# A hybrid attention and retention layer: rotated keys stored whole beside their halves, two key tiles moved behind the value tiles, and the order of two splits turned round

## The reference, cut to what matters

```
q = rotary(q.reshape(B, S, H, 256), positions)          # H = 4 retention heads
k = rotary(k.reshape(B, S, H, 256), positions) * 256 ** -0.5
v = v.reshape(B, S, H, 512)
def step(R, chunk):                                     # chunks of 128 tokens, 8 for each head
    qc, kc, vc = chunk
    inner = ((qc @ kc.T) * decay_in) @ vc
    cross = (qc @ R) * xi
    R = R * gamma_c + (kc * zeta).T @ vc                # needs the key with its tokens as rows
    return R, inner + cross
```

## Time and profile before

| what | value |
|---|---|
| time, median of 3 runs | 1659.99 us (1658.79 to 1666.12) |
| profiled execution, its own time | 1659.99 us |
| its span | 1658.2 us |
| TensorE busy | 1601.9 us (97%) |
| VectorE busy | 952.4 us (57%) |
| ScalarE busy | 583.6 us (35%) |
| GpSimd busy | 231.9 us (14%) |
| data moved | 300.72 MB, mean 181 GB/s |

### The profile page before, as it was taken

One profiled execution on the slowest core, in us unless ns is written; L12 is line 12 of the kernel. 1 busy time (PEld: TensorE's weight loads), 2 busy tenths in 40 slices (PEclk: granted clock), 3 DMA queues, 4 the chain that ended last, 5 costly groups with the idle time before them and its releaser, 6 DMA issues.

```text
span 1658.2 us, 20322 instructions
## 1 busy us (share of the span) xinstructions
PE 1601.9 (97%) x7788; PEld 1341.4 (81%) x7788; DVE 952.4 (57%) x1472; ACT 583.6 (35%) x1009; POOL 231.9 (14%) x180
## 2 busy tenths in 40 slices
PE   5999999999999999999999999999799999999998
PEld 4778888888888888888888888787588878888886
DVE  6984444444448766555565555655466665647544
ACT  5443333333343323233343433434243333212111
POOL 2232232222311221212000000000010010000000
PEclk8999999999999999999999999999899999999999
DMA  9032323322232558697564454557987786435322
GB/s 387 25 127 109 113 109 113 116 108 109 108 134 82 186 209 303 241 347 219 198 207 171 163 191 166 186 179 270 346 259 239 246 254 236 161 100 218 140 100 79
DMA packets 156240, 300.72 MB, mean 181 GB/s; under 512 B 10864, under 2 KB 95728, under 8 KB 148208
## 3 DMA queue, kind: packets, MB, share of 16 engines
q1 hardware_dynamic: 145344, 269.20, 46.8%
q0 software_dynamic: 4608, 16.78, 2.5%
q10 hardware_dynamic: 6192, 13.44, 2.5%
HBM read 191.90 MB, written 106.95 MB: 180 GB/s over the span
## 4 chain that ended last, share of the span: by engine, by line
PE 84%; DVE 8%; DMA 4%; ACT 2%; issue 2%; SPq 1%; POOL 0%; DVEq 0%; ACTq 0%; POOLq 0%
PE p_banks L2031 9%; PE p_banks L1989 8%; PE p_banks L1991 8%; PE p_banks L1992 8%; PE p_banks L2062 5%; PE p_banks L1904 5%; PE p_banks L1906 5%; PE p_banks L1905 5%; PE p_banks L2237 4%; PE p_banks L2235 3%; PE p_banks L2236 3%; PE p_banks L2296 2%; PE p_banks L2295 2%; PE p_banks L2294 2%; PE p_banks L2133 2%
## 5 line engine op out<-in xcount | busy, mean ns | idle before, releaser
L1509 DVE TENSOR_TENSOR w_form<-w_pair,w_form 128x512 fp32r<-128x512 f32 x120 | 92.9, 776 | 101.8 <-ACT w_form L1156 100.5
L1156 ACT ACTIVATE w_form<-w_pair 128x512 fp32r<-128x512 f32 x120 | 75.6, 632 | 195.3 <-PE p_banks L1992 187.3
L510 ACT ACTIVATE w_hi<-w_raw 128x1024 fp32r<-128x1024 f32 (+3 forms) x79 | 70.1, 889 | 208.9 <-PE p_banks L2237 99.7
L1904 PE MATMUL p_banks<-h_hi,w_hi 128*128 128x512 f32 x304 | 118.6, 390 | 1.6 <-DVE w_lo L516 1.6
L1905 PE MATMUL p_banks<-h_lo,w_hi 128*128 128x512 f32 x304 | 118.3, 389 | 0.0
L1906 PE MATMUL p_banks<-h_hi,w_lo 128*128 128x512 f32 x304 | 118.3, 389 | 0.0
L516 DVE TENSOR_TENSOR w_lo<-w_raw,w_hi 128x1024 fp32r<-128x1024 f32 (+3 forms) x80 | 92.0, 1154 | 31.9 <-ACT w_hi L510 31.5
L2237 PE MATMUL p_banks<-y_hi,w_lo 128*128 128x512 f32 x256 | 99.6, 389 | 0.0
L2236 PE MATMUL p_banks<-y_lo,w_hi 128*128 128x512 f32 x256 | 99.6, 389 | 0.0
L2235 PE MATMUL p_banks<-y_hi,w_hi 128*128 128x512 f32 x256 | 99.6, 389 | 0.0
L1224 ACT ACTIVATE prob<-p_banks,neg_max 128x128 f32<-128x128 f32 (+3 forms) x64 | 47.5, 742 | 144.4 <-DVE neg_max L1607 144.4
(11 more groups left out here) (293 smaller groups left out, 4303.6 us busy)
## 6 DMA issues: line engine op xcount, KB each, us to landing
w_raw<-in_w_dense SPq DMA_DIRECT2D x45, 512.0 KB, 5.3
w_pair<-in_w_pairs SPq DMA_DIRECT2D x20, 1024.0 KB, 4.9
v_ret<-v_stage POOLq DMA_DIRECT2D x32, 512.0 KB, 3.7
qk_chunk<-qk_chunks SPq DMA_DIRECT2D x32, 512.0 KB, 4.0
v_chunk<-v_ret SPq DMA_DIRECT2D x32, 512.0 KB, 4.6
qk_chunks<-split_stage SPq DMA_DIRECT2D x28, 512.0 KB, 5.9
merge_t<-act_t SPq DMA_DIRECT2D x48, 256.0 KB, 3.6
act_t<-stage SPq DMA_DIRECT2D x40, 256.0 KB, 2.0
```

The source lines that it names most:

```text
L1509: nc.vector.tensor_tensor(self.form[f % FORM_SLOTS][:, 1, :], self.form_source(f), self.form[f % FORM_SLOTS][:, 0, :].bitcast(F32), ALU.su ...
L1904: nc.tensor.matmul(out, w_hi[:, slot, cut], x_hi[:, k, tok], start=(k == ks[0]), stop=False)
```

## The change

Four things change.

1. The rotated key is also stored whole. `store_turned` issues for a key pair two more stores of 512 KB, of `rot[:,0]` before the halves of part 0 and of `rot[:,3]` before those of part 1; a chunk in `qk_chunks` has 10 blocks instead of 8, 640 KB instead of 512 KB. The next tile that writes `rot` waits on DVE until the stores of all key pairs so far have landed (`rot_stored`). SP waits for the same before it loads the first attention gate.
2. `sum_keys`, `k_chunk_full` and `KEY_SUMS` go; TensorE transposes blocks 8 and 9 of the loaded chunk.
3. `x10` and `x11` move behind `v3`: `... x9 k4 v0 k5 v1 k6 v2 k7 v3 x10..x15`. The loads of the first attention operands are issued after x11's stores instead of after v3's.
4. For `q` and `k` tiles ACT and DVE first split the result and then the weight of tile r+3; before it was the other way round.

```diff
@@ -77,8 +77,8 @@
 for n in range(4):
-    SEQ += [("k", 4 + n), ("v", n)] + [("x", 10 + n)] * (n < 2)
-SEQ += [("x", n) for n in range(12, TURNS)]
+    SEQ += [("k", 4 + n), ("v", n)]
+SEQ += [("x", n) for n in range(10, TURNS)]
@@ -108,7 +108,6 @@
-KEY_SUMS = {28: 2, 29: 3, 30: 6}
@@ -192,8 +191,7 @@
-        self.qk = z("qk_chunk", 56, [P, 3, 8, P], F32R)
-        self.k_full = z("k_chunk_full", 68, [P, 3, 2, P])
+        self.qk = z("qk_chunk", 56, [P, 3, 10, P], F32R)
...
@@ -405,7 +403,8 @@
             elif kind in "abx":
-                self.rot_pair[r] = rot // 4
+                self.rot_pair[r], self.k_turns[r] = rot // 4, turned
+                turned += kind == "x" and i % 4 == 3
@@ -673,10 +672,10 @@
-            if r == R_LAST_V + 2:
+            if r == R_LAST_V + 3:
...
@@ -702,6 +701,7 @@
         sp.wait_ge(self.w_lo_ready, R_V + V_PARTS)
+        sp.wait_ge(self.rot_stored, 16 * 2 * H_RET)
@@ -726,6 +726,11 @@
         for part in range(2):
+            if is_k:
+                sp.wait_ge(self.rot_added, 2 * self.rot_pair[r] + part + 1)
+                col = (8 + part) * P
+                sp.dma_start(dst[:, :, col:col + P], self.rot[:, 3 * part, :].rearrange("p (m n) -> p m n", m=NT))\
+                    .then_inc(self.rot_stored, 16)
             sp.wait_ge(self.split_lo_ready, s + part + 1)
...
@@ -1094,15 +1086,13 @@
             if kind in "qk":
-                self.split_weight(act, r + RING)
                 act.wait_ge(*self.done[r])
                 self.split_hi(act, self.splits[r], self.two_banks(r))
...
-            if kind not in "qk":
-                self.split_weight(act, r + RING)
+            self.split_weight(act, r + RING)
@@ -1395,6 +1385,8 @@
             dve.wait_ge(self.split_lo_ready, self.splits[before] + 2)
+            if self.k_turns[r]:
+                dve.wait_ge(self.rot_stored, 32 * self.k_turns[r])
@@ -1525,7 +1517,6 @@
             if kind in "qk":
-                self.lower_weight(dve, r + RING)
                 self.split_low(dve, self.splits[r], self.two_banks(r))
...
-            if kind not in "qk":
-                self.lower_weight(dve, r + RING + (r == R_V - 1))
+            self.lower_weight(dve, r + RING + (r == R_V - 1))
@@ -2141,11 +2131,11 @@
     def turn_keys(self, pe, n):
-        pe.wait_ge(self.k_summed, n + 1)
+        pe.wait_ge(self.chunk_loaded[n % 3], 16 * (n // 3 + 1))
...
-            last = self.nc.tensor.transpose(self.p[:, 5, b * P:(b + 1) * P], self.k_full[:, n % 3, b, :],
+            last = self.nc.tensor.transpose(self.p[:, 5, b * P:(b + 1) * P], self.qk[:, n % 3, 8 + b, :].bitcast(F32),
...
-            "qk": scratch("qk_chunks", (H_RET, NT, P, 8 * P)),
+            "qk": scratch("qk_chunks", (H_RET, NT, P, 10 * P)),
```

More of the change, by code:

```diff
@@ L305, in semaphores @@
         self.rot_added = sem("rot_added")
+        self.rot_stored = sem("rot_stored")
         self.split_stored = [sem("split_stored_%d" % n) for n in range(3)]
@@ L338, in semaphores @@
         self.gc_loaded = [sem("gate_chunk_loaded_%d" % n) for n in range(3)]
-        self.k_summed = sem("k_chunk_summed")
         self.k_turned = sem("k_turned")
@@ L393, in counts @@
         self.done, self.free, self.splits, self.store_count = {}, {}, {}, [0, 0, 0]
-        summed = evicted = split = rot = 0
-        self.rot_pair = {}
+        summed = evicted = split = rot = turned = 0
+        self.rot_pair, self.k_turns = {}, {}
         for r, (kind, i) in enumerate(SEQ[:R_MERGE]):
@@ L675, in sync @@
             kind, i = SEQ[r]
-            if r == R_LAST_V + 2:
+            if r == R_LAST_V + 3:
+                later = [s for s in self.slot_of if s >= self.splits[R_LAST_V + 2]]
                 for n in range(3):
-                    later = [s for s in self.slot_of if s >= self.splits[r] and self.slot_of[s] == n]
-                    sp.wait_ge(self.split_stored[n], self.stores_before[later[0]] if later else self.store_count[n])
+                    sp.wait_ge(self.split_stored[n], self.stores_before[[s for s in later if self.slot_of[s] == n][0]])
                     sp.wait_ge(self.v_up_stored[n], 16 * 4)
@@ L989, in gpsimd @@
                 nc.gpsimd.tensor_tensor(rot[:, 3, :], rot[:, 3, :], rot[:, 1, :], ALU.add).then_inc(self.rot_added, 1)
-        sums = 0
         for unit in range(FILL_UNITS):
-            while sums < KEY_SUMS.get(unit, 0):
-                self.sum_keys(pool, sums)
-                sums += 1
             self.store_fill(pool, unit)
[L996 to L1004, removed]
     def store_fill(self, queue, unit):
```

## The result

The changed kernel takes 1677.17 us (median of 5, 1675.96 to 1679.56), the kernel before 1659.94 (median of 5). The ratio is 1.010, 95% interval 1.008 to 1.012: 17.2 us slower. The forecast was 1671.6 with a range of 1662 to 1680, and slower by more than 0.5%. So the sign and the range held, and the size was 5.6 us short. The forecast's own band, 1667 to 1676, is missed by 1.2 us. That the wide range holds is luck: its upper end, 1680, was the price of a rival that did not occur.

The account below looks back on a forecast made before the run. TensorE, busy 1601.9 of 1658.2 us, was taken as the bound, so only its tile starts count. Terms of 6.4, 1.1, 2.2, 0.9 and 1.0 sum to 11.6 us on 1659.99: 1671.6 us, range 1662 to 1680.

Parts of the forecast that it names:

- The forecast's own band: Range given to the forecast case itself, 1667 to 1676 us, with chance 0.58.
- Part 1 at x4: Up stage: x4's rotary products wait for the whole-row store until 561.0, so x6 starts late; +6.4 us, bounds 4 to 10.
- wait of 2 us at q3: Up stage, expected sign: TensorE has new waits of about 2 us each before q1, q3 and a0.
- Part 4 at x8: Up stage: x8's high weight, now made after the split, delays its start; +1.1 us, bounds 0 to 2.
- Part 3: k and v in a row: v2 waits 3.1 us, v3's 1.8 us stall goes; +2.2 us, bounds -1.8 to +8.
- Part 1 at the end of the up stage: One more store in front of the first value load makes it land later; +0.9 us, bounds 0 to 1.9.
- Part 2: Retention's start: removed POOL sums gain 0, larger chunk loads delay the last set 0 load; +1.0 us, bounds 0 to 1.3.
- 6.4 + 1.1 + 2.2 + 0.9 + 1.0: Sum of the five terms over the whole kernel, 11.6 us slower.
- recovered in between: Rival: only 1 to 3 us remain at x6 and k and v in a row come out even; 1665 us, chance 0.20.
- bound by transfers: Rival: stores in the k and v run are not caught up, costing 8 us and more at x10, x11; 1680, chance 0.15.
- not slower: Rival: the whole-row store lands by 555.5, costing nothing, and -1.8 us remains at v3; 1658 us, chance 0.07.
- signs named beforehand: Expected if right: x4 near 561, x6 6.4 us late, v2 waiting 3 us, v3 none, y_lo waits 1 longer.

Follow-up runs that it names:

- Run 4: The change, with the whole-row store of rot[:,3] issued by ScalarE on its own queue; 1668.64 us, ratio 1.0077 to the kernel before.
- run 6: The change, with spare products that nobody reads on TensorE before q1 and before v2's fifth tile; 1675.6 us, ratio 1.0102 to the kernel before.
- Run 2: The kernel before with only k and v in a row, x10 and x11 moved behind v3; 1662.03 us, ratio 1.0036.
- run 1: The kernel before with only the split put before the weight for q and k tiles; 1659.19 us against 1657.72, ratio 1.0008.
- run 7: The kernel before with x10 behind v1, x11 behind v2, and set 0's loads in front of the next chunk loads; 1653.78 us against 1659.19, ratio 0.997.
- run 8: The kernel before with only set 0's loads issued in front of the next chunk loads; 1653.79 us against 1657.69, ratio 0.9976.
- run 3: The change without k and v in a row and without split before weight; 1670.11 us, ratio 1.0082 to the kernel before.
- run 5: The change, with attention's first value load in front of the last key pair's stores; 1671.42 us against 1659.19 for the kernel before, ratio 1.0074.
- run 9: The kernel before with whole keys stored, no sums, and the edits of Run 4, run 5 and run 7; 1658.9 us against 1657.69, ratio 1.0005.

## Why the prediction was right, and where it fell short

**Part 1 at x4: right within 0.3 us.** The store behind both halves of part 0 lands 6.4 us after its issue, and DVE sits idle until then:

```profile
561.24 2.36 DVE L1395 TENSOR_TENSOR rot<-p_banks,ret_tables_back 128x1024 f32<-128x1024 f32 x2 [6.30 <-DMA qk_chunks<-rot]
563.51 0.55 DVE L515 TENSOR_TENSOR w_lo<-w_raw,w_hi 128x384 fp32r<-128x384 f32 x1
```

The forecast had 561.0 for the product, 563.9 for q1, 579.9 for a0 and 588.6 for x6; they are 561.24, 564.12, 580.05 and 588.82. Run 4 brings the landing forward and the delay goes with it. (The estimate by the line rate of the Trainium skill, DMA: Bandwidth & Descriptors, Specifications, had made this term 4.4; the measured landing speaks against it.) One detail was wrong: no wait of 2 us at q3, as slow matmuls had filled it (run 6).

**Part 4 at x8: right**, 1.1 us forecast, 1.2 in the change, 1.35 alone.

**Part 3: right in place, 1.6 us short.** v2 waits 2.81 us (forecast 3.1) and v3 0.84 (0.4), v3's old stall is gone, but from x8 to x12 the delay grows by 3.8 us, not 2.2. Behind v2's wait its remaining 24 matmuls take 4.36 us (694.73 to 699.09) instead of 2.87, so 1.5 us is the lower clock. But run 6, which held the clock up there, started x10 no sooner, so how much of the shortfall is the clock's stays open. Run 2 shows the same 3.9 without the other parts. (The forecast's four waits, 3.1, 0.3, 0.3 and 0.4, sum to 4.1, not 4.0.)

**Part 1 at the end of the up stage: the term that failed.** Forecast +0.9, measured 4.3 (11.6 to 15.9). I counted the place in SP's queue, 1.9 us, and there it is: the load is issued at 788.2, 13.4 us later than before, while TensorE is 11.6 late. But its time to landing grew too, from 9.4 to 11.1:

```profile
L754 SPq DMA_DIRECT2D v_head<-v_hl x1: 1815/1815/1815, 788.2 to 788.2; - x1
...
DMA to landing us min/median/max: 11.1/11.1/11.1
```

Two stores of GpSimd's follow 1.0 us behind it, and both land before it:

```profile
L1000 POOL DMA_DIRECT2D v_ret<-v_stage x2: 539/646/754, 789.2 to 789.9; - x2
...
DMA to landing us min/median/max: 6.4/7.3/8.3
```

In the kernel before they were issued 2.9 us behind the load, and landed behind it. By the Trainium skill (DMA: Bandwidth & Descriptors, Queues, rings and completion order) each transfer engine takes packets in turn from the queues that have work; the trace agrees, as the later stores land first. That this pairing lengthened the landing is the likeliest reading, and the other traces go with it: where GpSimd's stores follow 2.8 to 3.0 us behind the load (before, runs 1, 2, 7 and 8) it lands after 9.4 or 9.5 us, where 2.1 us behind (run 4) after 9.7, and where 1.0 us behind (the change, runs 3 and 6) after 11.1, 11.2 and 12.2. But the last three are also those with a whole-row store among the four issued just in front of the load, and only the whole step was tested (run 5). With the slack of 1.0 the wait is 2.5, and the clock fell behind it: 1.7 us more.

**Part 2: right in size.** The waits for `y_lo` grew by 1.4 us, against 1.0. Over the runs, those with wide chunks and the loads in their old order have 12.3, 12.2, 12.5, 11.7 and 11.9, those with narrow ones 10.9, 11.7 and 10.2. The groups touch at 11.7. That taking away POOL's sums gave something back shows in no trace of the change.

**The sum.** The step that failed is "6.4 + 1.1 + 2.2 + 0.9 + 1.0": it priced each stall by its idle time alone. Added idle time is 10.1 us against 11.6 forecast; the other 6.7 us are busy time that the sum has no term for. Some 5.9 of them are the lower clock: the busy time of each microsecond from 50 us on, times what its granted clock lacks of the upper level, sums to 16.16 us in the change and 10.25 before. Neither is additive along the program: between 790 and 1126 the change gets 2.6 us back, 0.6 of it in the stall before 1069 (1.93 us before, 1.30 after), behind which only the kernel before shows a low clock. Near 1380 it loses 1.4 by one more such stretch. The rival "recovered in between" was wrong for the up stage, and "bound by transfers" as well: no gap over 2 us at k6, k7 or x10. The rival "not slower" fell: with the landing at 551.7 + 3.5 = 555.2, within its condition of 555.5, the change is still 0.8% above before (run 4), and what the rival had missed first is the next key pair. Level it comes only in run 9, without part 4 and with further edits, of which one alone gives 0.24% (run 8). Of the signs named beforehand, v3 was to have no wait and had 0.84 us.

## What to carry to other kernels

Price a stall of TensorE at its idle time and then ask what clock is granted behind it: here 1.5 to 3.0 us of slower matmuls came on top of most waits of 2.1 to 2.9 us (of one of 2.79 none), and cost that much unless a later release decided anyway. The kernel before shows such a stall (956), and the surcharge can be read there. When a store is added to a queue, ask for each load behind it not only how much later it is issued, but also what other queues' transfers it now starts beside. And where loads for two stages share a full queue, the one that is needed first goes first: that reordering gave 0.24% by itself, while no part of this change gave anything.

## What the runs showed of the hardware

- The granted clock fell behind single stalls of 2.31, 2.48 and 2.81 us in the change and of 2.92 in run 2, and not behind those of 0.84, 1.00 and 1.31 in the change and 1.62 (717) before. The length alone does not decide: it fell behind 1.67 us (1077.85, run 4) and 1.93 (1069, before), but not behind 1.81 (1080.80, run 3) or 2.79 (956.52, run 9). Groups of short stalls differ from run to run too: after one of 1.10 us and one of 0.4 near 1380 it fell in the change and not behind 1.10 and 0.64 in the kernel before.
- Keeping TensorE busy with unread products held the clock at its upper level (run 6), and bought nothing where another engine's chain sets the next release.
- Stretches that are mostly stores in rows of 512 bytes moved 272 GB/s before and 283 in the change, with the transfer engines' share at 0.93 and 1.00, while stretches of other stores and loads reached 400 to 424 at about the same share.
